# The block scheme with seven products also in the third feed-forward block, behind an RMS norm whose scale is known only in its first group

## The reference

```python
h = rms_norm(x, ffn2_pre_g)                     # x * rsqrt(mean(x*x) + 1e-6) * g
gate, up = jnp.split(h @ ffn2_w_in, 2, axis=-1) # 1024 -> 2 x 2816
x = x + 0.5 * rms_norm((jax.nn.silu(gate) * up) @ ffn2_w_out, ffn2_post_g)
```

## Time and profile before

| | |
|---|---|
| median of 3 runs | 2826.27 us (2824.88 to 2830.18) |
| profiled execution, its own time | 2823.89 us |
| its span, first to last instruction | 2822.1 us |
| granted TensorE clock, mean | 0.999 |
| PE busy | 2790.5 us, 99% |
| DVE, ACT, POOL busy | 1660.6, 1145.4, 608.1 us |
| group 2 of f2 starts at | 656.26 us |
| block groups of a0, b0, a1, b1 start at | 1021.58, 1584.36, 1939.64, 2500.92 us |

### The profile page before, as it was taken

The page is one execution under the profiler, slowest core; times in us unless marked ns, Lnnn a source line. Parts: engine busy times, 40 slices in busy tenths (PEclk is TensorE's granted clock), DMA queues, the critical chain, the costliest instruction groups (busy, mean ns, idle before and its releaser), DMA issues.

```text
span 2822.1 us, 41432 instructions
## 1 busy us (share of the span) xinstructions
PE 2790.5 (99%) x17221; PEld 2431.1 (86%) x17221; DVE 1660.6 (59%) x2285; ACT 1145.4 (41%) x1561; POOL 608.1 (22%) x641
## 2 busy tenths in 40 slices
PE   9999999899999999999999999999999999999999
PEld 8888887678888899988878999889998887899987
DVE  5544443554433378854656788547885465678853
ACT  5233244643322354433435544335443343554432
POOL 0114626301110031110142311113111014231110
PEclk9999999999999999999999999999999999999999
DMA  4232223122223357722213576235772221357632
GB/s 152 97 97 97 90 75 103 50 80 93 97 97 98 103 137 183 176 97 83 90 49 101 141 184 171 98 99 140 184 175 98 82 90 53 96 144 183 169 100 80
DMA packets 119114, 319.71 MB, mean 113 GB/s; under 512 B 16848, under 2 KB 16976, under 8 KB 118928
## 3 DMA queue, kind: packets, MB, share of 16 engines
q1 hardware_dynamic: 98192, 279.32, 30.2%
q0 software_dynamic: 20736, 37.76, 9.0%
HBM read 313.74 MB, written 2.10 MB: 112 GB/s over the span
## 4 chain that ended last, share of the span: by engine, by line
PE 92%; DVE 3%; ACT 2%; issue 1%; DMA 1%; POOL 0%; SPq 0%; ACTq 0%; DVEq 0%; POOLq 0%
PE bank L401 18%; PE bank L403 18%; PE bank L402 18%; PE bank L589 8%; PE bank L593 8%; PE bank L591 8%; PE bank L538 2%; PE bank L418 1%; PE bank L424 1%; PE bank L419 1%; PE bank L467 1%; PE bank L471 1%; PE bank L468 1%; PE bank L548 1%; DMA praw<-weight_pairs 1%
## 5 line engine op out<-in xcount | busy, mean ns | idle before, releaser
L1638 DVE TENSOR_TENSOR wlo<-wraw,whi 128x1024 fp32r<-128x1024 f32 x327 | 427.0, 1318 | 437.3 <-ACT whi L1016 437.0
L1016 ACT ACTIVATE whi<-wraw 128x1024 fp32r<-128x1024 f32 x335 | 348.5, 1054 | 476.7 <-DMA wraw<-weights 476.6
L401 PE MATMUL bank<-H,whi 128*128 128x512 f32 x1096 | 429.9, 392 | 1.3 <-DVE H L1761 0.7
L403 PE MATMUL bank<-H,whi 128*128 128x512 f32 x1096 | 426.6, 389 | 0.0
L402 PE MATMUL bank<-H,wlo 128*128 128x512 f32 x1096 | 426.6, 389 | 0.0
L401 PE MATMUL bank<-Ah,whi 128*128 128x512 f32 x1056 | 412.8, 391 | 0.0
L403 PE MATMUL bank<-Al,whi 128*128 128x512 f32 x1056 | 411.0, 389 | 0.0
L402 PE MATMUL bank<-Ah,wlo 128*128 128x512 f32 x1056 | 410.9, 389 | 0.0
L589 PE MATMUL bank<-TF,plo 128*128 128x256 f32 x1152 | 326.0, 283 | 0.0
L591 PE MATMUL bank<-TF,phi 128*128 128x256 f32 x1152 | 326.0, 283 | 0.0
L593 PE MATMUL bank<-TF,phi 128*128 128x256 f32 x1152 | 326.0, 283 | 0.0
(11 more groups left out here) (350 smaller groups left out, 5002.0 us busy)
## 6 DMA issues: line engine op xcount, KB each, us to landing
wraw<-weights SPq DMA_DIRECT2D x335, 512.0 KB, 3.4
praw<-weight_pairs SPq DMA_DIRECT2D x144, 384.0 KB, 4.7
praw<-weight_pairs SPq DMA_DIRECT2D x144, 256.0 KB, 3.8
praw<-weight_pairs POOLq DMA_DIRECT2D x144, 256.0 KB, 4.5
X<-x_t SPq DMA_DIRECT2D x8, 256.0 KB, 6.8
y_t<-X SPq DMA_DIRECT2D x8, 256.0 KB, 2.1
dist<-attention SPq DMA_DIRECT2D x4, 256.0 KB, 4.3
wraw<-weights SPq DMA_DIRECT2D x2, 256.0 KB, 4.3
```

What stands on the lines that cost most here:

```text
L401: pe.matmul(b, sh, mh, start=start, stop=False)
L403: signal(pe.matmul(b, sh, ml, start=False, stop=stop), keys)
L1016: act.activation(whi[:, u % NS, :], wraw[:, u % NS, :], ACT.Copy).then_inc(*S.done("weights_hi", ("hi", u)))
L1638: dve.tensor_tensor(wlo[:, u % NS, :], wraw[:, u % NS, :], f32(whi[:, u % NS, :]), SUB).then_inc(*S.done("weights_lo", ("lo", u)))
```

## The change

`f2` joins `PAIRED`, with three plain groups (`PLAIN`) ahead of eight block groups. The block form adds and subtracts halves of the tokens, so it needs rows that already hold the factor of each token. In the first group DVE writes the fully scaled rows (x, gain and `Rb`) into `Xn`, which lies in the part of `Af` that later groups fill. POOL makes the token sums from `Xn` in the second group. In the third group, as soon as the plain matmuls have used two rows of `H`, ACT and DVE write the high and low parts of the scaled rows over them. The first output rows of f2 are made two at a time (`two_rows`), as in the other block stages. POOL's list of f2 now holds transfers, gates and token sums. The core of the diff:

```diff
-PAIRED = ("a0", "b0", "a1", "b1")
-N_PAIRS = (NF // 2 - 2) * 4
+PAIRED = ("f2", "a0", "b0", "a1", "b1")
+PLAIN = {"f2": 6, "a0": 4, "b0": 4, "a1": 4, "b1": 4}
+N_PAIRS = {st: (NF - PLAIN[st]) * 2 for st in PAIRED}
+PAIR_AT = {st: sum(N_PAIRS[o] for o in PAIRED[:i]) for i, st in enumerate(PAIRED)}
...
-for _name, _n in (("f1", FFN_TILES), ("f1 out", OUT_TILES), ("m1", MIX1), ("m1 out", MIX1_OUT), ("f2", FFN_TILES),
+for _name, _n in (("f1", FFN_TILES), ("f1 out", OUT_TILES), ("m1", MIX1), ("m1 out", MIX1_OUT), ("f2", FIRST_TILES + 4 * KD),
...
-    ffn_in("f2_in", "f2_in", NF)
-    rows("f2_out", NF, KD)
+    for j in range(0, PLAIN["f2"], 2):
+        groups(("f2_in",) * 4, (j, j + 1, NF + j, NF + j + 1))
+    two_rows("f2_out")
...
+    Xn = Af[:, NF - KD:NF, :]
...
+        return (2, q, 3, 1 - q)[s % 4], ((q, 2, 1 - q) if st == "f2" else (q, 1 - q, 2))[s % 3]
...
+                    if i == 0 and first and st == "f2":
+                        pe.wait_ge(*S.at(("normed lo", st, 2 * k + 1)))
...
+        def ffn_rms_pairs(st):
+            p = START[st]
+            for j in (0, 2, 4):
+                for k in range(KD):
+                    hi_to(p + 16 * j + 4 * k + 3, plain_end(st) - 1)
+                    if j == 0:
+                        rms_mid(st, k)
+                    if j == 4:
+                        act.wait_ge(*S.at(("unit", plain_end(st) - 4 + k // 2)))
+                        act.wait_ge(*S.at(("normed", st, k)))
+                        act.activation(Hh[:, k, :], Xn[:, k, :], ACT.Copy).then_inc(
+                            *S.done("moving_hi", ("normed hi", st, k)))
+                        if k % 2 == 0:
+                            token_hi(st, k // 2)
+                        if k == 5:
+                            raw_hi(PAIR_AT[st])
+                            sum_hi(PAIR_AT[st])
+                for i in range(2):
+                    act.wait_ge(*S.at(("gate in", st, j + i)))
+                    act.activation(tmp[i], tmp[i], ACT.Silu).then_inc(*S.done("silu", ("silu", st, j + i)))
+                if j == 2:
+                    for i in range(KEPT):
+                        split_a(st, i)
+            raw_hi(PAIR_AT[st] + 1)
+            sum_hi(PAIR_AT[st] + 1)
+            raw_hi(PAIR_AT[st] + 2)
+            block_groups(st)
...
+        def block_groups(st):
+            n, v0 = N_PAIRS[st], PAIR_AT[st]
+            for j in range(PLAIN[st], NF, 2):
                 for k in range(4):
-                    s = 2 * (j - 4) + k
-                    if k == 0 and 0 < s < N_PAIRS - 2:
+                    s = 2 * (j - PLAIN[st]) + k
+                    if k == 0 and 0 < s < n - 2:
                         raw_hi(v0 + s + 2)
...
+                    if st == "f2":
+                        if s == n - 1:
+                            act.wait_ge(*S.at(("pair unit", v0 + n - 2)))
+                            hi(plain_end(st))
+                            hi(plain_end(st) + 1)
+                    else:
...
+        def ffn_rms_pairs(st):
+            p = START[st]
+            v0 = PAIR_AT[st]
+            for j in (0, 2, 4):
+                for k in range(KD):
+                    lo_to(p + 16 * j + 4 * k + 3, plain_end(st) - 1)
+                    if j == 0 and k == KD - 2:
+                        rms_recip(st, (st, "rms"))
+                    if j == 4:
+                        dve.wait_ge(*S.at(("normed hi", st, k)))
+                        dve.tensor_tensor(Hl[:, k, :], Xn[:, k, :], f32(Hh[:, k, :]), SUB).then_inc(
+                            *S.done("moving_lo", ("normed lo", st, k)))
+                        if k % 2 == 0:
+                            token_lo(st, k // 2)
+                        if k == 5:
+                            more_sums(v0)
+                            pair_lo(v0)
+                            sum_lo(v0)
+                if j == 4:
+                    more_sums(v0 + 1)
+                dve.wait_ge(*S.at(("full", (st, j))))
+                if j == 0:
+                    dve.wait_ge(*S.at(("Rb", st)))
+                for i in range(2):
+                    if j:
+                        dve.wait_ge(*S.at(("product", st, j - 2 + i)))
+                    dve.tensor_tensor(tmp[i], bank(((st, j), i))[:, :], Rb[:, :], MUL).then_inc(
+                        *S.done("gates", ("gate in", st, j + i), empties=[((st, j), i)]))
+                if j == 0:
+                    dve.wait_ge(*S.at(("H free", "m1o")))
+                for i in range(2):
+                    dve.wait_ge(*S.at(("gate", st, j + i)))
+                    dve.tensor_tensor(Af[:, j + i, :], bank(((st, j), 2 + i))[:, :], tmp[i], MUL).then_inc(
+                        *S.done("gates", ("product", st, j + i), empties=[((st, j), 2 + i)]))
+                if j == 0:
+                    for k in range(KD):
+                        dve.scalar_tensor_tensor(Xn[:, k, :], X[:, k, :], c("g_f2pre", k), Rb[:, :], MUL, MUL).then_inc(
+                            *S.done("rows", ("normed", st, k)))
+                if j == 2:
+                    for i in range(KEPT):
+                        split_a(st, i)
+            pair_lo(v0 + 1)
+            sum_lo(v0 + 1)
+            block_groups(st)
...
+        def ffn_rms_pairs(st):
+            v0 = PAIR_AT[st]
+            add_pairs(v0)
+            add_pairs(v0 + 2)
+            gates(st, 0, 2)
+            for k in range(4):
+                token_sums(st, k, Xn, ("normed", st, 2 * k + 1))
+            gates(st, 2, 4)
+            add_pairs(v0 + 1)
+            gates(st, 4, 6)
+            more_pairs(st)
...
-        def gates(st):
-            for j in range(NF):
+        def gates(st, j0, j1):
+            for j in range(j0, j1):
...
-        gates("f2")
+        ffn_rms_pairs("f2")
...
             for st in PAIRED:
-                if u == START[st] // 8 + 3:
+                if u == plain_end(st) - 5:
                     load_pair(st, 0)
-                if u == START[st] // 8 + 5:
+                if u == plain_end(st) - 3:
                     load_pair(st, 2)
-                if u == START[st] // 8 + 7:
+                if u == plain_end(st) - 1:
                     load_pair(st, 1)
-                    for s in range(3, N_PAIRS):
+                    for s in range(3, N_PAIRS[st]):
                         load_pair(st, s)
```

More of the change, by code:

```diff
@@ L118, in pair_plan @@
     plan = []
+    parts = {"f2": (("f2_in", 0), ("f2_in", NF))}
     for l in range(2):
[L120 to L124, removed]
+        for st, n in (("a", 1), ("b", 2)):
+            parts[f"{st}{l}"] = ((f"gate{n}_{l}", 0), (f"up{n}_{l}", 0))
+    for st in PAIRED:
+        for j in range(PLAIN[st], NF, 2):
+            for k in range(4):
+                for kk, jj in ((2 * k + 1, j + 1), (2 * k, j), (2 * k + 1, j), (2 * k, j + 1), (2 * k, j + 1)):
+                    plan.extend((name, kk, base + jj) for name, base in parts[st])
     return plan
@@ L568, in pair_group @@
         def pair_group(st, j):
-            v0 = PAIRED.index(st) * N_PAIRS + (j - 4) * 2
+            first = j == PLAIN[st]
+            v0 = PAIR_AT[st] + (j - PLAIN[st]) * 2
             use = (st, j)
@@ L582, in pair_group @@
                         pe.wait_ge(*S.at(("pair lo", v)))
-                    if form == 3 and j == 4:
+                    if i == 0 and first and st == "f2":
+                        pe.wait_ge(*S.at(("normed lo", st, 2 * k + 1)))
+                    if form == 3 and first:
                         pe.wait_ge(*S.at(("TF", st, k)))
@@ L602, in ffn @@
             if st in PAIRED:
-                gemm_group((st, 0), st, (), None, idle)
-                gemm_group((st, 2), None)
-                for j in range(4, NF, 2):
+                for j in range(0, PLAIN[st], 2):
+                    gemm_group((st, j), None if j else st, (), None if j or not rms else rms_mid(st), 0 if j else idle)
+                for j in range(PLAIN[st], NF, 2):
                     pair_group(st, j)
@@ L1019, in raw_hi @@
             raw, hi_slot = pair_slots(v)
-            s = v % N_PAIRS
-            u0 = START[PAIRED[v // N_PAIRS]] // 8
+            st, s = pair_step(v)
             act.wait_ge(pair_in[raw], 16 * pair_landings(v))
[L1023 to L1026, removed]
+            if s < 3 and hi_slot == 2:
+                act.wait_ge(*S.at(row_done(st, KD - 1)))
+            elif s < 3:
+                act.wait_ge(*S.at(("unit", plain_end(st) - (3 if s == 0 else 1))))
             else:
@@ L1693, in ffn_pairs, with block_groups @@
+        def block_groups(st):
+            n, v0 = N_PAIRS[st], PAIR_AT[st]
+            for j in range(PLAIN[st], NF, 2):
                 for k in range(4):
-                    s = 2 * (j - 4) + k
-                    if 0 < s < N_PAIRS - 1:
+                    s = 2 * (j - PLAIN[st]) + k
+                    if 0 < s < n - 1:
                         more_sums(v0 + s + 1)
@@ L2423, in vector_program @@
         mixer_1()
-        ffn("f2", True, (("H free", "m1o"),))
```

(8 more changed lines are left out.)

105 lines of the change are left out of this document (56 added, 49 removed).

## The result

The changed kernel takes 2842.68 us (median of 4 runs, 2840.57 to 2845.5) against 2825.9 us: ratio 1.0061, 95% interval 1.0047 to 1.0075. It is 16.8 us slower, where 12.0 us were forecast; the median lies inside the range. The profiled execution has its own time of 2845.5 us, with a span of 2843.7 us, at the upper end of the runs.

What follows compares the result with a forecast made beforehand. PE, busy 99% of the span, was taken as the bound. Terms -12.8 + 17.6 + 1.7 + 5.5 = +12.0 us gave 2835.9, and with the median 2.4 us higher 2838.3 us (0.42% slower); range 2832.0 to 2846.0.

Steps and rivals of the forecast that it cites:

- rival 2: DVE and POOL wait for whole instructions of each other in f2's second group: stall 20.4 us, total +14.8, 2841.1 us; chance 0.15.
- the first stall: f2's second group: POOL's gates wait behind an adding transfer, delaying DVE's low part; PE stands 17.6 us from 645.38.
- the second stall: End of f2's third group: PE waits for DVE's gate, product and low part in the first pair units, 5.5 us.
- The gain: Eight f2 groups in block form take 20.16 instead of 21.76 us each on PE: 12.8 us less.
- Crowding: f2's second group: POOL's token sums slow DVE 1.46 times, six scaled rows at 0.96 us, low part 1.72 us.
- The clock: Behind PE's long wait in f2, 3.4 us at half clock, 1.7 us lost.
- Outside f2: The other stages were to stay unchanged, no cost.
- the waits of the block groups: Waits inside f2's eight block groups, costed at nothing; 0 to 1.5 us kept for the range.
- The rival with the gates not held: f2's gates run beside POOL's waiting transfer: -7.2 us, 2819.1, chance 0.05; or -4.2, 2822.1, no change, chance 0.05.
- that of half the loss: In f2, quicker landing, no slowing, clock stays high: +5.2 us, 2831.5 us; chance 0.05.

Runs made afterwards that it cites:

- the rearranged kernel: Changed kernel with DVE's low parts ahead of scaled rows, POOL's gates first, third group's end reordered: 2816.19 and 2816.93 us, 0.9965 and 0.9971 of the kernel before.
- The moved line: Changed kernel with POOL's adding transfer for pair unit 2 moved from ahead of the first gates to behind the token sums: 2829.31 us, 1.0013 of the kernel before.
- the early transfer: Changed kernel with SP issuing pair unit 2's transfers right behind those of pair unit 0, POOL's list kept: 2831.7 us, 1.0021 of the kernel before.

## Why the prediction was right, point by point

The sign, the main chain and the place were right. The forecast was 4.8 us short in the medians, and the total of 16.8 is nearer to rival 2's 14.8; but that rival's stall of 20.4 us was not there. In the first profile f2's 15.9 us are -12.8, 18.05 for the first stall, 2.3 for the clock behind it, 4.9 for the second stall, 1.7 for the clock behind that, and 1.4 of waits in the block groups, which leaves 0.4 unplaced.

- **The gain** (12.8 us): not visible in the changed kernel by itself, but its block groups took 169.32 and 166.41 us with waits and half clock in them, and the rearranged kernel took 163.17 against 161.3 us. Right, less about 2 us of waits. The output rows in pairs of two cost nothing, as assumed: from the end of the last hidden group to a0 it is 125.8 us before and 125.9 in the changed and in the rearranged kernel.
- **The first stall** (17.6 us): 18.05 us over the pitch, 17.89 us of idle time. Landing 4.0 (4.1 forecast), gates 0.6 behind the start of POOL's issue (0.9), products 3.5 us behind the gates' start (3.27), eight rows 7.6 from the first to the low part (7.1 forecast), low part 1.7. The moved line shows that POOL's list is the cause, the early transfer that it is the landing that the list waits for.
- **Crowding**: the size was near, the mechanism was not, and the nearness is luck. I had scaled durations by 1.46: two rows at 0.66 and six at 0.96. Measured were three at 0.66 and five at 1.13. POOL's first sum began just behind the third row, and from then on rows and sums started in turn, one of each. What an operation of DVE loses to a sum is about 0.5 us whatever its length, not a share of it: 0.47 for a row, 0.53 for a low part. The factor of 1.46 for the differences of the earlier trace rows was a mean over both kinds too: the two took 0.68 and 1.05 us. Rival 2 had taking turns right and its price too high: 1.40 for a row and 1.92 for a low part, where 1.13 and 1.67 were measured. The Trainium skill ("SBUF — State Buffer", section "Who interferes with whom") states such a lock for the whole instruction. The trace agrees with it in the turns; in the price it does not, since a row and a sum take 0.66 and 0.70 us alone and 1.13, not 1.36, together.
- **The clock** (1.7 us): too small. The low stretch behind the return lasted 4.92 us in the window shown, and costs 2.3 us by the two windows of 145 matmuls. In the other two profiles of the changed kernel it was 5.57 and 4.38 us. I had taken the length of one stretch after an idle time of 2 us for that after 17.
- **The second stall** (5.5 us): gaps over the pitch of 2.04, 1.23 and 1.29 us and 0.3 us at the start, 4.9 in all, each released by the instruction named. The order of events was right, and the waits 0.6 us shorter. What I left out is that a second half clock follows these waits in some executions: a low stretch of 3.4 us, 1.7 us lost, in two of three profiles.
- **Outside f2** (nothing): the three profiles are 5.7, 1.7 and 8.2 us longer there than that of the kernel before, whose time is 2.0 us under its median. In the first profile f2 starts 1.3 us late already: a stretch at 407 us stood at half clock that was at full clock in the kernel before, and the change had not begun there. The three medians over before, 14.9, 16.8 and 18.8 us, lie 0.9 to 2.7 us above f2's own 13.3, 15.9 and 16.1. Whether these 1 to 3 us belong to the change stays open.

The term that was mis-sized most is thus the clock, 1.7 us where 2.3 to 4.0 are lost, and next to it the waits of the block groups, 0 where 0.2 to 1.4 were found. The rival with the gates not held is excluded by the profile, in which the first gate starts at 651.79, and that of half the loss by the medians. Rival 2 is excluded in its price, not in its shape.

## What to carry to other kernels

When work is added to an engine's list, look at what each of its waits holds up behind it: here a transfer whose weights ACT first read at 707.70, 56 us behind its issue, stood ahead of two gates that were needed at once, and the chain over three engines turned a gain of 12.8 us into a loss. Sort each list by when its results are needed, not by which stage they belong to; after that, the same work gained 10 us. And price a long stall with its clock: the time behind it counts too. When two engines crowd each other, read single rows and not a mean over crowded and free ones.

## What was not expected of the hardware

- Behind 17.9 us of idle time PE worked 4.4 to 5.6 us at half clock, behind 5.5 us still 4.3 us and behind 7.8 us 3.1 us; behind 1.81 us not at all. But three waits of 1.1 to 1.9 us within 5 us were followed by 3.4 us of half clock in two of three profiles of the changed kernel.
- Beside a stream of POOL's sums of 128x256, DVE's operations started in turn with them and each took about 0.5 us more, one of 0.66 us as well as one of 1.14. But a single sum that started beside DVE's low parts took 3.91 us instead of 0.74 and did not slow them.
- The same transfer landed 1.5 us later in both kernels with extra matmuls in the long wait, for a reason not found.
